# A chunked state scan: the second side of a triangular inverse made by VectorE block transposes instead of TensorE products

## The reference, cut to what matters

```
def step(S, inp):
    rt, vt, wt, kt, at, bt = inp
    sa = einsum('bhij,bhj->bhi', S, at)
    S = S * wt[:, :, None, :] + sa[..., None] * bt[:, :, None, :] + vt[..., None] * kt[:, :, None, :]
    return S, einsum('bhij,bhj->bhi', S, rt)
s_end, ys = lax.scan(step, s0, xs, reverse=reverse)
```

## Time and profile before

| | |
|---|---|
| runs of the kernel before | 3787.69, 3774.82, 3781.83 us |
| median | 3781.83 us |
| span of the profiled execution, first to last instruction | 3780.2 us |
| the scan in it | about 2799 to 3440 us |
| PE busy over the span | 3524.4 us, 93% |
| mean granted PE clock | 0.982 |

### The profile page before, as it was taken

The page is one execution under the profiler, slowest core; times in us unless marked ns, Lnnn a source line. Parts: engine busy times, 40 slices in busy tenths (PEclk is TensorE's granted clock), DMA queues, the critical chain, the costliest instruction groups (busy, mean ns, idle before and its releaser), DMA issues. The chain is left out here.

```text
span 3780.2 us, 60072 instructions
## 1 busy us (share of the span) xinstructions
PE 3524.4 (93%) x24875; PEld 1824.6 (48%) x24875; DVE 2048.1 (54%) x3270; ACT 698.6 (18%) x1383; POOL 563.2 (15%) x809
## 2 busy tenths in 40 slices
PE   6999998999989998999999999989998899888998
PEld 2354443334544445554444444543356676665443
DVE  1699983352356776557646566436533334344435
ACT  2100001122210111431100000335622222221000
POOL 0111111120000002000000110631113223332100
PEclk9999999999999999999999999999999999999999
DMA  9989995982244467335477686558854333335663
GB/s 366 333 302 330 344 347 208 330 326 77 73 183 175 175 239 263 106 126 202 166 257 255 227 326 229 167 190 273 266 158 152 107 104 112 105 100 181 240 223 111
DMA packets 362625, 799.01 MB, mean 211 GB/s; under 512 B 26630, under 2 KB 73790, under 8 KB 357746
## 3 DMA queue, kind: packets, MB, share of 16 engines
q1 hardware_dynamic: 259760, 459.54, 35.5%
q0 software_dynamic: 72992, 274.20, 20.1%
q10 hardware_dynamic: 29602, 61.42, 4.3%
HBM read 686.90 MB, written 108.18 MB: 210 GB/s over the span
## 5 line engine op out<-in xcount | busy, mean ns | idle before, releaser
L1228 PE MATMUL gemm_a_g_ps<-store_w,turned 128*128 128x512 f32 (+1 forms) x1152 | 457.6, 560 | 2.7 <-PEq L108 2.7
L759 DVE SCALAR_TENSOR_TENSOR pmods_acc<-pmods_w,cond,pmods_acc 128x512 f32<-128x512 f32 x540 | 384.4, 749 | 23.6 <-issue 0.5
L1228 PEld LDWEIGHTS gemm_a_g_ps<-store_w,turned 128*128 128x128 f32 x1152 | 209.4, 191 | 250.3 <-issue 250.3
L3084 PE MATMUL scan_g_ps<-store_w,turned 64*64 64x512 f32 x2048 | 288.1, 610 | 10.5 <-DVE outlet_stage L3098 6.8
L1228 PE MATMUL att_a_g_ps<-store_w,turned 128*128 128x512 f32 x512 | 240.2, 599 | 6.9 <-ACT outlet_stage L2812 4.2
L1228 PE MATMUL feat_g_ps<-store_w,turned 128*128 128x512 f32 x384 | 181.9, 622 | 14.6 <-ACT outlet_stage L2240 12.4
L1275 PE MATMUL out_c_g_ps<-store_w,turned 128*128 128x512 f32 x384 | 167.6, 592 | 0.0
L1228 PE MATMUL tail_g_ps<-store_w,tail_branch_t 128*128 128x512 f32 x384 | 165.7, 592 | 0.9 <-ACT tail_branch_t L3913 0.9
L3449 DVE TENSOR_TENSOR scan_tm<-scan_tm,scan_ps 128x256 f32<-128x256 f32 x128 | 53.8, 421 | 168.8 <-PE scan_ps L3337 168.6
L1228 PEld LDWEIGHTS att_a_g_ps<-store_w,turned 128*128 128x128 f32 x512 | 91.5, 191 | 100.0 <-issue 93.4
L3337 PE MATMUL scan_ps<-scan_tmt,scan_y 64*64 64x64 f32 x2560 | 118.9, 223 | 14.2 <-issue 10.7
(11 more groups left out here) (577 smaller groups left out, 5934.0 us busy)
## 6 DMA issues: line engine op xcount, KB each, us to landing
store_w<-in_w_in SPq DMA_DIRECT2D x160, 1024.0 KB, 7.9
pmods_w<-in_w_mod POOLq DMA_DIRECT2D x40, 2048.0 KB, 13.2
store_w<-in_a_w_in SPq DMA_DIRECT2D x48, 1024.0 KB, 10.9
store_w<-in_c_w_in SPq DMA_DIRECT2D x40, 1024.0 KB, 8.4
first_mods_w<-in_w_mod SPq DMA_DIRECT2D x32, 1024.0 KB, 14.3
store_w<-in_a_w_out SPq DMA_DIRECT2D x32, 1024.0 KB, 6.2
scan_raw<-s_feat SPq DMA_DIRECT2D x112, 256.0 KB, 4.5
s_feat<-feat_o POOLq DMA_DIRECT2D x16, 1536.0 KB, 7.9
```

Of the source, the lines that this page charges most:

```text
L759: v.scalar_tensor_tensor(a, src, x, a, ALU.mult, ALU.add)
L1228: mm = pe.matmul(to, lhs, self.store.slot[i % self.store.NS][:, k, :width], start=first, stop=last)
L3084: mm = pe.matmul(self.ps[r][halves[o], :], self.act_tile(k, tb)[halves[r], halves[o]], self.store.slot[i % self.store.NS][halves[r], k % 4 ...
```

## The change

TensorE computes only the inverse's transpose. VectorE makes the inverse from it with a transpose of 32x32 blocks, which is a full transpose as long as T's blocks are no larger than 32 (k < 5), and T itself is not needed after k = 5. All matrices stay on their own partitions, so nothing is crossed. The identity is added to `y1` on VectorE, which makes `level` give the whole new `tmt` rather than what is to be added to it; ScalarE copies it. The diff, cut to its core:

```diff
-                "dve": ["ft", "at", "ak"] + ["rk"] * lat + [f"{a}{k}" for k in levels for a in ("t", "tt")][:-2] + [f"tt{N_LEVELS}"] + ["pm", "m1", "m2"],
-                "act": ["ft", "av"] + [f"half{k}" for k in levels] + ["tz", "outer"] + ["y"] * lat,
-                "pool": ["eye"] + [f"lt{k}" for k in levels] + ["dg"],
+                "dve": ["ft", "at", "ak", "t0"] + ["rk"] * lat + [f"{a}{k}" for k in levels for a in ("y", "t")][:-1]
+                + ["pm", "m1", "m2"],
+                "act": ["ft", "av"] + [f"tt{k}" for k in levels] + ["tz", "outer"] + ["y"] * lat,
+                "pool": [f"lt{k}" for k in levels] + ["dg"],
...
                 inner(d, AT, 1, 0)
-                inner(d, A_, 0, 1, cross=True)
-                odd_crossed(d, 1, 0)
                 mm = inner(d, AK, 2, 0)
...
             def half(k):
                 def f(d, g, s, lat):
                     after(pe, d, "pool", g, s, f"lt{k}")
-                    if k > 1:
-                        after(pe, d, "dve", g, s, f"t{k - 1}")
-                    elif lat:
-                        after(pe, d, "dve", g, s, "rk")
-                    for h, c, where in by_quadrant:
-                        src = chunks[where]
-                        mm = pe.matmul(crossed(d, 0, 1)[chunks[c], h % 2, h // 2, :], lt[d][src, k - 1, h, :],
-                                       tm[d][src, h, :], start=True, stop=True)
+                    after(pe, d, "dve", g, s, "rk" if lat and k == 1 else f"t{k - 1}")
+                    for h in range(HG):
+                        for c in chunks:
+                            mm = pe.matmul(quarter(d, 0, 0)[c, h, :], lt[d][c, k - 1, h, :], tm[d][c, h, :], start=True, stop=True)
...
             def level(k):
                 def f(d, g, s, lat):
-                    after(pe, d, "act", g, s, f"half{k}")
-                    if k > 1:
-                        after(pe, d, "dve", g, s, f"tt{k - 1}")
...
+                    after(pe, d, "dve", g, s, f"y{k}")
+                    after(pe, d, "act", g, s, f"tt{k - 1}" if k > 1 else "av")
+                    for h in range(HG):
                         for c in chunks:
+                            mm = pe.matmul(quarter(d, 2, 1)[c, h, :], y1[d][c, h, :], tmt[d][c, h, :], start=True, stop=True)
...
             def tz_(d, g, s, lat):
-                after(pe, d, "dve", g, s, f"tt{N_LEVELS}")
+                after(pe, d, "act", g, s, f"tt{N_LEVELS}")
...
             def at_(d, g, s, lat):
                 after(v, d, "pe", g, s, "products")
-                a_t, a = product(d, AT), product(d, A_)
-                strict = masks[:, d, STRICT, :].unsqueeze(1).broadcast_to([P, HG // 2, HD])
-                v.tensor_tensor(by_parity(at[d])[:, 0, :, :], a_t[:, 0, :, :], strict, ALU.mult)
-                v.tensor_tensor(by_parity(at[d])[:, 1, :, :], quarter(d, 2, 0)[:, 0:HG // 2, :], strict, ALU.mult)
+                a_t = product(d, AT)
                 v.tensor_tensor(by_parity(tmt[d]), a_t, mask_by_parity(d, FIRST), ALU.mult)
-                v.tensor_tensor(by_parity(tm[d]), a, mask_by_parity(d, FIRST_T), ALU.mult)
+                v.tensor_tensor(by_parity(at[d]), a_t, mask_by_parity(d, STRICT), ALU.mult)
                 v.drain()
                 v.sem_inc(dve_done[d], 1)
+
+            def t0(d, g, s, lat):
+                v.tensor_tensor(tmt[d][:, :, :], tmt[d][:, :, :], eye, ALU.add)
+                v.drain()
+                v.transpose(tm[d][:, :, :], tmt[d][:, :, :]).then_inc(dve_done[d], 1)
...
+            def y_(k):
+                def f(d, g, s, lat):
+                    after(v, d, "pe", g, s, f"half{k}")
+                    v.tensor_tensor(y1[d][:, :, :], quarter(d, 0, 0), eye, ALU.add).then_inc(dve_done[d], 1)
+                return f
+
             def t_(k):
                 def f(d, g, s, lat):
                     after(v, d, "pe", g, s, f"level{k}")
-                    v.tensor_tensor(by_parity(tm[d]), by_parity(tm[d]), crossed(d, 0, 0), ALU.add).then_inc(dve_done[d], 1)
-                return f
...
+                    v.transpose(tm[d][:, :, :], quarter(d, 2, 1)).then_inc(dve_done[d], 1)
                 return f
...
-                order = [("ft", 0), ("ft", 1), ("at", 0), ("ak", 0), ("at", 1), ("ak", 1)]
-                order += [(stage, d) for stage in names[3:] for d in range(2)]
+                order = [("ft", 0), ("ft", 1), ("at", 0), ("ak", 0), ("at", 1), ("ak", 1), ("t0", 0), ("t0", 1)]
+                order += [(stage, d) for stage in names[4:] for d in range(2)]
...
             for k in levels:
-                run[f"half{k}"] = copies(f"half{k}", lambda d, lat, x: [(by_parity(y1[d]), crossed(d, 0, 1))])
+                run[f"tt{k}"] = copies(f"level{k}", lambda d, lat, x: [(tmt[d][:, :, :], quarter(d, 2, 1))], f"t{k}" if k < N_LEVELS else None)
...
                     after(pool, d, "dve", g, s, "at")
-                    pool.tensor_tensor(tm[d][:, :, :], tm[d][:, :, :], eye, ALU.add)
-                    pool.tensor_tensor(tmt[d][:, :, :], tmt[d][:, :, :], eye, ALU.add).then_inc(pool_done[d], 1)
                     pool.tensor_tensor(lt[d][:, 0, :, :], at[d][:, :, :], mask(d, FIRST + 1), ALU.mult).then_inc(pool_done[d], 1)
```

More of the change, by code:

```diff
@@ L3265, in turned, with inner @@
                 mm.then_inc(pe_done[d], 1)
-            def inner(d, o, x, y, cross=False):
+            def inner(d, o, x, y):
                 for hp in range(0, HG, 2):
                     for h, to in ((hp, 0), (hp + 1, 1), (hp, 1), (hp + 1, 0)):
[L3271 to L3281, removed]
+                        mm = pe.matmul(product(d, o)[chunks[to], h % 2, h // 2, :], head(ft[d], h, x)[:, chunks[to]],
+                                       head(ft[d], h, y)[:, chunks[to]], start=True, stop=True)
                 return mm
@@ L3324, in f @@
                 def f(d, g, s, lat):
-                    after(pe, d, "act", g, s, f"half{k}")
-                    if k > 1:
-                        after(pe, d, "dve", g, s, f"tt{k - 1}")
[L3329 to L3335, removed]
-                        for c in chunks:
[L3337 to L3342, removed]
-                            update_t(h + 1)
-                            update_tt(h)
-                            mm = update_tt(h + 1)
-                    else:
-                        for h in range(HG):
-                            mm = update_tt(h)
+                    after(pe, d, "dve", g, s, f"y{k}")
+                    after(pe, d, "act", g, s, f"tt{k - 1}" if k > 1 else "av")
+                    for h in range(HG):
+                        for c in chunks:
+                            mm = pe.matmul(quarter(d, 2, 1)[c, h, :], y1[d][c, h, :], tmt[d][c, h, :], start=True, stop=True)
                     mm.then_inc(pe_done[d], 1)
@@ L3417, in _ @@
             v.wait_ge(tables, 64)
+            eye = eye2[:, :].unsqueeze(1).broadcast_to([P, HG, HD])
             def ft_(d, g, s, lat):
@@ L3448, in f @@
                     after(v, d, "pe", g, s, f"level{k}")
-                    v.tensor_tensor(by_parity(tm[d]), by_parity(tm[d]), crossed(d, 0, 0), ALU.add).then_inc(dve_done[d], 1)
-                return f
-            def tt_(k):
-                def f(d, g, s, lat):
-                    after(v, d, "pe", g, s, f"level{k}")
-                    v.tensor_tensor(tmt[d][:, :, :], tmt[d][:, :, :], quarter(d, 2, 1), ALU.add).then_inc(dve_done[d], 1)
+                    v.transpose(tm[d][:, :, :], quarter(d, 2, 1)).then_inc(dve_done[d], 1)
                 return f
@@ L3472, in m_ @@
                 return f
-            run = {"ft": ft_, "at": at_, "ak": ak, "rk": rk, "pm": pm_, "m1": m_(0), "m2": m_(1)}
+            run = {"ft": ft_, "at": at_, "ak": ak, "t0": t0, "rk": rk, "pm": pm_, "m1": m_(0), "m2": m_(1)}
             for k in levels:
-                run[f"t{k}"], run[f"tt{k}"] = t_(k), tt_(k)
-            made_by = {"ft": "turned", "at": "products", "ak": "products", "pm": "outer", "m1": "chain1", "m2": "chain2"}
-            made_by.update({f"{a}{k}": f"level{k}" for k in levels for a in ("t", "tt")})
+                run[f"y{k}"], run[f"t{k}"] = y_(k), t_(k)
+            made_by = {"ft": "turned", "at": "products", "ak": "products", "t0": "products", "pm": "outer", "m1": "chain1", "m2": "chain2"}
+            made_by.update({f"{a}{k}": f"{b}{k}" for k in levels for a, b in (("y", "half"), ("t", "level"))})
             t = 0
@@ L3498, in _, with copies @@
         def _(act):
-            def copies(name_of_product, pairs):
+            def copies(name_of_product, pairs, turned_first=None):
                 def f(d, g, s, lat):
                     after(act, d, "pe", g, s, name_of_product)
+                    if turned_first:
+                        after(act, d, "dve", g, s, turned_first)
                     for dst, src in pairs(d, lat, raw[s % 2][d]):
@@ L3527, in _ @@
                     for d in range(2):
```

(2 more changed lines are left out.)

4 lines of the change are left out of this document (2 added, 2 removed).

## The result

The changed kernel takes 3731.3 us (median of 4 runs, 3728.35 to 3734.4), the kernel before 3783.6 beside it: ratio 0.987, 95% interval 0.9855 to 0.9884. The forecast was 3762 us with a range from 3742 to 3788: the direction was right, the gain of 52 us was two and a half times the forecast of 20, and the range missed it.

A forecast was written before the change was run, and what follows sets the result against it. PE, busy 93% of the span, was taken to set the scan's time, partly waiting for code. Levels -4.5, products -11.7, VectorE +4 and stalls -8 gave -20.2 us: 3781.8 to 3761.6, say 3762 us, range 3742 to 3788.

The forecast's parts named there:

- The levels: Scan's `half` and `level` cycles with their units and waits: -4.6, -5.4, +3.8 and +1.7 us, together -4.5 us.
- The products: Non-latent `products` on PE: 24 of 56 records go, 0.367 us at each of 32 places, -11.7 us.
- VectorE's queue: `rk` behind `t0` delays `half1`, +2.4 us; adding up two finished tiles before `y`, 0.8 us each; together +4 us.
- POOL: Drops two operations of 0.725 us for each of 32, 46 us in all, hidden under units and `av`: no gain.
- The issue stalls: PE waiting for code in the scan: 22 fewer instruction packets, taken as -8 us, between nothing and -20.
- The end of the range: Largest stall gain considered, -20 us: 17.5% of 115 us, if each round lost 7.2 us.
- the two rounds above: Rounds with the same stages and 870 matmuls each, 32.5 and 39.7 us, read as stalls growing with DMA traffic.
- 1 and 2: Rivals on VectorE's transpose: 0.69 us long, 3775 us, 15%; or it becomes the bound, 3842 us at 1.18 us, 8%.
- slack sum: In the levels, each transpose costs twice its excess over 0.42 us at 40 counts, over 0.66 us at 96 more.
- The bank rule: Rival: row tiles cannot share a PSUM bank, so `half` costs 1.78 us a pair; 3815 us, 3%.
- 311 ns: Skill's figure for VectorE's 128x128 bf16 transpose; doubling columns put the new one under 0.62 us, losing at most 8 us.

The follow-up runs named there:

- e3: The changed kernel with the 12 removed products of each `products` stage computed again, result unread: 3742.1 us, ratio 0.99 to the kernel before.
- e6: The changed kernel with every projection unit issued as twice as many products of half as many columns: 3750.5 us, ratio 0.9922 to the kernel before.
- e5: The changed kernel with `half` spread over all four quarters again, the odd heads' inverse not computed: 3718.3 us, ratio 0.9833 to the kernel before.
- e7: The kernel before with `half` on two quarters only, same number of instructions, the odd heads' inverse not computed: 3791.7 us, ratio 1.0028.
- e12: The changed kernel with a second VectorE transpose ahead of the one in each level: 3739.7 us, ratio 0.9887 to the kernel before.
- e4: The changed kernel with the 8 products of T's update computed again in every level for k below 5, result unread: 3776.7 us, ratio 0.9997 to before.

## Why the prediction missed

**The levels, -4.5 us.** Right in its walk, 3.5 us too small. Free cycles: unit after `level` 3.24 to 3.00 at 32 places (-7.7), pairs 6.90 to 6.66 at 16 (-3.8), k = 5 +0.15 at 12 and +0.42 at 4 (+3.5): -8.0 us. Most of the difference is in the first term, since 3.19 was read at k = 1, the shortest.

**The products, -11.7 us.** Right: `products` and `rk` together 79.7 to 68.3 us of free time, -11.4, and e3.

**VectorE's queue, +4 us.** Right in size, +4.6, but not where I put it: `av` 30.1 to 31.7 free, and the units' waits for a finished tile 5.2 to 8.2 us (L3098 in the groups), since `t0` stands ahead of the adding up; I had looked for that ahead of `y`. The small waits for `y` and `tm` (3.5 and 4.8 us) replace those for ACT and DVE of before (7.5, 3.5 and 4.0). POOL: nothing, as said.

**The issue stalls, -8 us: this is the step that failed.** I read correctly that they were PE waiting for code, and priced them in proportion to the code that went, 0.28 us for each of 22 packets. They measured -31 us by the issue rows, 1.4 us a packet, four times that term of the sum. By e6 a packet costs 1.2 us in these levels; by e5 and e7 pace alone moves the stalls by 10 to 16 us with the same code. The change did two things at once there: it took a third of the levels' records, and it spread those of `half` over twice the time. The end of the range was wrong too: -20 came from the two rounds above, whose difference was mostly a wait for VectorE.

With -8.0, -11.4, +4.6 and -31.3 the sum is -46.1, against the 57.1 us by which the scan shrank and the 52 us measured on the whole kernel. Of the 11 us that are missing in the scan, up to some 8 can be the clock, which the forecast did not have: in the scan of before the granted clock fell from 2.4 to 1.2 GHz in seven stretches, in after in two. All seven began during a PE wait of 1.2 us or more, or at most 1.4 us behind one. One cost at most 1.7 us, an estimate from the row above with a mean of 0.85 over 11.05 us. The rest is open. The excess fell by 43.7 us, but some 4 of these are free time of before that was read too small, where the fastest followed a stall.

**The rivals.** The transpose: 0.449 us, so 1 and 2 did not arise, and e12 shows that their slack sum was several times too dear. The bank rule of the Trainium skill (TensorEngine Tiling (Array Packing), Restrictions and Gotchas) does not show as a cost here: `half` writes one bank from both row tiles and a pair takes 0.83 us, not 1.78. The Trainium skill's 311 ns for a transpose of half the columns in bf16 (VectorE: DVE Perf Modes, The three transpose paths) gave an estimate of under 0.62 us; the trace has 449 ns for 256 columns of float32, which lies under it.

## What to carry to other kernels

Where PE issues many small matmuls, look at "issue" first, and count the records between two stalls: if they come in multiples of 251 to 254, PE is waiting for its own code, and the transfers of the instruction queue say so directly: here PE went on 1.2 to 1.6 us after one had ended. Then what a removed instruction is worth depends on where it stood: in the levels' long runs of small matmuls it was worth its array time and half as much again (e4: 45 us for 29), in `products`, ahead of long matmuls, its array time alone (e3). And a stage that became slower on the array while the code stayed the same cost less than its length (e7).

## What the hardware showed that was not expected

- With the DMA moving 226 to 377 GB/s, PE got its next 16 KB of code 6.9 to 7.7 us after it had begun on the last. The transfer itself took 1.0 to 1.1 us of that; it began only 4.6 to 5.1 us after PE had.
- A stall can cost more than itself: after those of 2.16 us at 3253.6 and 2.25 us at 3260.5 the granted clock, 1.00 before, had a mean of 0.85 over the next 11 us, a part of them at 1.2 GHz and the rest at 2.4. Over the whole scan it was 0.98 before and 0.99 after.
- VectorE transposes 128x256 float32 in 449 ns, from PSUM or SBUF, near the 424 ns of an addition of that size.
- A slower `half` (e7) cost under half of its array time.

That PE waits for packets of its code is shown by the counts, by the transfers of the instruction queue, and by the runs on pace and traffic. That one packet at a time is fetched ahead is worked out from the times of one trace and was not tried. What else delays one in a round with little traffic stays open, and so does how much of the gain is less code and how much is slower pace.
